# Summing six chunks of squares elementwise before the tensor engine's norm reduction, and loading the root table earlier

## The reference, cut to what matters

```python
def rmsnorm(x, g):
    xf = x.astype(jnp.float32)
    y = xf * lax.rsqrt(jnp.mean(xf * xf, axis=-1, keepdims=True) + NORM_EPS)
    return (y * g.astype(jnp.float32)).astype(x.dtype)

    # per layer l of 2
    h = rmsnorm(x, P['norm1_g'][l]) * (1 + sc1) + sh1
    y = mixer(h)
    x = x + gt1 * y
    h = rmsnorm(x, P['norm2_g'][l]) * (1 + sc2) + sh2
    x = x + gt2 * moe(h, ...)
    # at the end
    y = rmsnorm(x, P['final_g'])
```

## Time and profile before

| what | value |
|---|---|
| median of 3 runs | 1816.75 us (1816.57 to 1817.38) |
| profiled execution, span from its first to its last instruction | 1813.6 us |
| median of the runs less that span | 3.15 us |
| PE busy | 1696.4 us, 94% of the span |
| DVE busy | 861.0 us, 47% |
| ACT busy | 280.8 us, 15% |
| GpSimd busy | 112.4 us, 6% |
| root activations of norms 1, 2, 3, 4 start at | 277.52, 841.25, 1240.05, 1804.23 us |

### The profile page before, as it was taken

The page is one execution under the profiler, slowest core; times in us unless marked ns, Lnnn a source line. Parts: engine busy times, 40 slices in busy tenths (PEclk is TensorE's granted clock), DMA queues, the critical chain, the costliest instruction groups (busy, mean ns, idle before and its releaser), DMA issues.

```text
span 1813.6 us, 25634 instructions
## 1 busy us (share of the span) xinstructions
PE 1696.4 (94%) x9272; PEld 971.4 (54%) x9272; DVE 861.0 (47%) x2513; ACT 280.8 (15%) x645; POOL 112.4 (6%) x115
## 2 busy tenths in 40 slices
PE   5999998999999999988999888878999999999996
PEld 2664576544444444435776877756544444444443
DVE  3206425455545554435672664335445554555444
ACT  2134313100100010003112112102100010001001
POOL 0000001000000000000000322000100000000000
PEclk9999789999999999998999899779999999999998
DMA  9967853699999999994331000033889999999993
GB/s 390 335 257 298 319 209 134 228 421 419 420 419 417 409 419 420 419 406 168 124 132 70 1 1 1 3 150 121 307 338 419 419 420 411 407 419 419 420 420 135
DMA packets 81235, 528.08 MB, mean 291 GB/s; under 512 B 13104, under 2 KB 13632, under 8 KB 20400
## 3 DMA queue, kind: packets, MB, share of 16 engines
q1 hardware_dynamic: 68256, 496.14, 67.0%
q0 software_dynamic: 9024, 20.03, 3.0%
q10 hardware_dynamic: 3824, 10.20, 1.6%
HBM read 533.04 MB, written 5.86 MB: 297 GB/s over the span
## 4 chain that ended last, share of the span: by engine, by line
PE 84%; DMA 8%; DVE 4%; issue 2%; ACT 1%; POOL 0%; SPq 0%; ACTq 0%; DVEq 0%
PE ps L665 21%; PE ps L463 14%; PE ps L709 12%; PE ps L692 11%; DMA ring<-in_wexp 4%; DMA arena<-in_wexp 3%; PE ps L649 3%; PE ps L426 3%; PE ps L612 2%; DVE arena L1267 2%; PE ps L922 1%; PE ps L435 1%; PE ps L925 1%; PE ps L443 1%; PE ps L532 1%
## 5 line engine op out<-in xcount | busy, mean ns | idle before, releaser
L1273 DVE SCALAR_TENSOR_TENSOR x<-ps,mod,x 128x256 f32<-128x256 f32 (+1 forms) x1024 | 329.1, 363 | 189.3 <-PE ps L709 120.3
L665 PE MATMUL ps<-arena 128*32 128x512 f32 (+2 forms) x1456 | 309.1, 609 | 8.4 <-DMA arena<-in_wexp 8.3
L709 PE MATMUL ps<-arena 128*128 128x288 f32 x960 | 264.8, 417 | 6.4 <-DVE x L1273 4.2
L709 PEld LDWEIGHTS ps<-arena 128*128 128x128 f32 x960 | 172.0, 189 | 139.6 <-issue 94.2
L665 PE MATMUL ps<-ring,arena 128*64 128x512 f32 (+1 forms) x976 | 211.4, 597 | 2.1 <-DMA arena<-in_wexp 2.1
L463 PE MATMUL ps<-h,ring 128*128 128x288 f32 x768 | 196.5, 417 | 2.1 <-ACT h L1022 2.1
L463 PEld LDWEIGHTS ps<-h,ring 128*128 128x128 f32 x768 | 149.0, 195 | 45.5 <-issue 4.2
L665 PEld LDWEIGHTS ps<-arena 128*32 128x32 f32 (+2 forms) x1456 | 92.6, 128 | 150.7 <-issue 150.2
L1267 DVE TENSOR_TENSOR arena<-ps,arena 128x256 f32<-128x256 f32 (+6 forms) x153 | 56.1, 373 | 211.5 <-issue 171.6
L692 PE MATMUL ps<-ring,arena 128*64 128x512 f32 (+2 forms) x624 | 134.4, 620 | 11.2 <-DMA ring<-in_wexp 11.2
L1590 DVE COPY arena<-ps 128x512 f32<-128x512 f32 x60 | 41.5, 692 | 172.2 <-PE ps L692 167.0
(11 more groups left out here) (273 smaller groups left out, 1640.1 us busy)
## 6 DMA issues: line engine op xcount, KB each, us to landing
arena<-in_wexp SPq DMA_DIRECT2D x210, 1024.0 KB, 23.3
ring<-in_wexp SPq DMA_DIRECT2D x180, 1024.0 KB, 23.1
ring<-in_wmod SPq DMA_DIRECT2D x48, 1024.0 KB, 9.6
ring<-in_win SPq DMA_DIRECT2D x26, 1024.0 KB, 4.9
ring<-in_wout SPq DMA_DIRECT2D x8, 1024.0 KB, 4.8
h_rows<-arena ACTq DMA_DIRECT2D x4, 512.0 KB, 2.6
x<-in_x ACTq DMA_DIRECT2D x1, 1152.0 KB, 16.1
out_y<-h SPq DMA_DIRECT2D x2, 576.0 KB, 2.8
```

Source lines behind the costliest of these rows:

```text
L665: last = mm(ps[2][w, :], xgT[:, r % 2, 4 * q + k, w], unit(("gu", l, s0 + i, q))[:, k * 512:(k + 1) * 512], start=(q == 0 and k == 0), sto ...
L709: mm(ps[ADD_BANKS[c]][:, 0:T], yb[:, r % 2, c * 128:(c + 1) * 128], onehot[:, r % 2, :], start=True, stop=True).then_inc(sem["add_ps"], 1)
L1273: return V.scalar_tensor_tensor(out=o, in0=a, scalar=s, in1=b, op0=op0, op1=op1)
```

## The change

There are two edits.

1. In norms 1 to 4 the squares of chunks 0 to 5 (`SUMMED = 6`) are added elementwise into `rms`, and PE reduces three operands in place of eight: first `rms`, then the squares of chunks 6 and 7. In norms 1 and 3 the five additions are made by DVE, each behind the square of its chunk in `residual`. In norms 2 and 4 GpSimd makes them, behind its last fetch; each waits for the square of its chunk and, from the second on, for its own previous addition (semaphore `sqp`). The fifth raises `sqa`, for which PE waits.
2. In norms 2 and 4 the root's table load moves from behind the eight squares on ACT to ahead of them. In norms 1 and 3 it stays.

```diff
+SUMMED = 6
@@
             def sum_squares(k):
 
-                for c in range(KC):
+                if k:
+                    pe.wait_ge(sem["sqa"], k)
+                    mm(ps[SS_BANK[k]][:, 0:T], ones, rms[:, :], start=True, stop=False)
+                for c in range(SUMMED if k else 0, KC):
                     pe.wait_ge(sem["sq"], KC * k + c + 1)
-                    last = mm(ps[SS_BANK[k]][:, 0:T], ones, h[:, c, :], start=(c == 0), stop=(c == KC - 1))
+                    last = mm(ps[SS_BANK[k]][:, 0:T], ones, h[:, c, :], start=(k == 0 and c == 0), stop=(c == KC - 1))
                 last.then_inc(sem["ss"], 1)
@@ ACT
             def norm_root(k):
-                if k:
+                if k in (1, 3):
                     warm(ACT.Sqrt)
@@ ACT, end of moe(l)
+                warm(ACT.Sqrt)
                 for c in range(KC):
                     act.wait_ge(sem["add_x"], KC * (B + NR - 1) + c + 1)
                     A(h[:, c, :], x[:, c, :], ACT.Square).then_inc(sem["sq"], 1)
@@ DVE, residual
                     square(i)
+                    if 0 < i < SUMMED:
+                        dve.wait_ge(sem["sq"], KC * (2 * l + 1) + i + 1)
+                        L(tt(rms[:, :], h[:, 0, :] if i == 1 else rms[:, :], h[:, i, :], ALU.add),
+                          "sqa" if i == SUMMED - 1 else None)
@@ GpSimd, end of moe(l)
+                for c in range(1, SUMMED):
+                    po.wait_ge(sem["sq"], KC * (2 * l + 2) + c + 1)
+                    if c > 1:
+                        po.wait_ge(sem["sqp"], (SUMMED - 2) * l + c - 1)
+                    po.tensor_tensor(rms[:, :], h[:, 0, :] if c == 1 else rms[:, :], h[:, c, :], ALU.add)\
+                        .then_inc(sem["sqp" if c < SUMMED - 1 else "sqa"], 1)
```

More of the change, by code:

```diff
@@ L155 @@
 SLOT, NTH, BEFORE = slots_of(UNITS)
-SEMS = """ld_small ld_rest ld_att ld_state st_mix st_small st_out w_used mod_row mod_t cond lamn lame lam sq ss rms hs h
+SEMS = """ld_small ld_rest ld_att ld_state st_mix st_small st_out w_used mod_row mod_t cond lamn lame lam sq sqa sqp ss rms hs h
  proj_ps proj_ev v_ps v_ev v_ev0 pad conv hst gate_ps gate_e lru_a lru_w ya
```

## The result

| | changed kernel | kernel before, same chip |
|---|---|---|
| median of the runs | 1811.01 us (6 runs, 1807.59 to 1812.35) | 1816.66 us (6 runs, 1815.28 to 1818.4) |
| ratio, with its 95% interval | 0.9965 [0.9954, 0.9975] | |
| span of the profiled execution | 1810.6 us | 1813.6 us |
| PE busy | 1688.5 us | 1696.4 us |

The change makes the kernel faster, as forecast. The ratio puts the gain at 1816.75 x 0.0035 = 6.4 us where 4.5 were expected (the two medians are 5.65 apart), with an interval from 4.5 to 8.4 us that just reaches the forecast. The time that the ratio gives, 1810.4 us, is at the low end of the range that was stated. The profiled execution took 1812.35 us for a span of 1810.6. That shifts no difference, only the way from span to run.

The account below looks back on a forecast made before the run. The prediction put the reduction on the path in all four norms, PE itself the limit in norms 1 and 3. Gains of 3.8 and 0.7 us took the median from 1816.75 to 1812.25 us, range 1810.4 to 1815.4.

Parts of the forecast that it names:

- Norms 1 and 3: PE limits the reduction; five matmuls fewer, DVE's additions free, eighth square late next: 1.9 us gained each, 3.8 together.
- Norms 2 and 4: GpSimd's addition chain, then three matmuls: 0.35 us gained each, 0.7 together; bounds per norm 0.8 loss to 0.7 gain.
- The gap between two dependent additions: On GpSimd in norms 2 and 4: taken as 0.09 us, with 0.38 as the upper bound.
- the six entries: PE's three matmuls behind GpSimd's sum in norms 2 and 4: 1.70 us.
- rival C: Clock behind norms: low stretch comes and ends earlier, 1810.75 us, chance 0.11; or one stretch is added, 1813.85, 0.06.
- The sum: All terms: span 1813.6 - 3.8 - 0.7 = 1809.1 us; median 1816.75 - 4.5 = 1812.25, 0.25% less.
- What carries to the end: Work behind the norms, including the MoE weight stream, moves with them, so their gains reach the end.
- Rival B: GpSimd's chain in norms 2 and 4 has gaps near 0.38 us, losing 0.8 each: 1814.55 us, chance 0.12.
- Rival D: Gain of norms 1 and 3 swallowed in the MoE by the weights' stream; only 0.7 stays: 1816.05 us, chance 0.05.
- Rival E: GpSimd and DVE block each other in norms 2 and 4, 2.8 us later each: 1818.55 us, chance 0.04.
- The table load: Root's load on ACT in norms 2 and 4: already hidden, moving it ahead of the squares gains nothing and costs 0.

Follow-up runs that it names:

- pool_norms: Kernel before with GpSimd's sums in norms 2 and 4 only, table load ahead of the squares there; 1816.61 us (11 runs), ratio 0.9995.
- again: The changed kernel run once more, unaltered; 1809.48 us (7 runs), ratio 0.9957 to the kernel before.
- table_behind: The changed kernel with the root's table load back behind the eight squares in all norms; 1809.37 us in one run.
- before_look: The kernel before, without an edit, run for one more trace; 1815.17 us in one run, beside 1817.0 for the kernel before.
- norm3_only: Kernel before with DVE's sum in norm 3 only; 1813.96 us (12 runs), ratio 0.9983.
- dve_norms: Kernel before with DVE's sum in norms 1 and 3 only, table load behind the squares; 1809.27 us (5 runs), ratio 0.9950.
- norm1_only: Kernel before with DVE's sum in norm 1 only; 1813.95 us (12 runs), ratio 0.9984.
- sum_five: Changed kernel, but in norms 2 and 4 GpSimd sums five chunks and PE takes squares 5, 6, the sum, then 7; 1810.10 us, repeated 1808.82.

## Why the prediction was right and wrong

**Norms 1 and 3: right, to 0.04 us.** Forecast 1.94 and 1.93, taken as 1.9; measured 1.90 in each, in every trace that has the sum there. What was named as late next, the eighth square, is what PE waits for (0.26 us), and the root starts 277.76 - 276.46 = 1.30 us behind that square's start. DVE's additions cost nothing: they lie in its idle time, as said, of which 2.25 us are left behind an addition.

**Norms 2 and 4: the right picture with the wrong numbers.** This is one of two terms that were mis-sized: forecast a gain of 0.7, measured 0.13 - 0.31, a loss of 0.18, in the first trace, a gain of 0.04 and a loss of 1.0 in the two repeats, and a gain of 0.25 in `pool_norms`. Two parts of it can be told apart. The gap between two dependent additions is 0.14 to 0.15 us and not the 0.09 of the row behind ACT: five additions take 4.55 us (833.91 to 838.46), not 4.31. That takes 0.24 of the 0.35 in each norm, and `pool_norms`, where nothing else is off, has 0.12 to 0.13 left. The other part is the six entries, forecast at 1.70. In the ten norms of this form they took 1.72 us five times (norm 2 of the first trace, norm 2 of `again`, both in `pool_norms`, norm 4 of `table_behind`) and 1.93 to 2.49 us the other five times, among them 2.16 in norm 4 of the first trace. The granted clock of that one shows it:

```profile
1797.00:1799.00 2.00, 0.01 (x1) 0.01 (x1) 1.06 (x4) 1.10 (x3) 1.65 (x3) 1.00 0.00 0
1799.00:1801.20 2.20, 2.15 (x6) 1.12 (x6) 0.00 (x0) 0.01 (x1) 0.00 (x0) 0.76 0.00 0
```

The clock falls from 1.00 to a mean of 0.76 just behind the two microseconds in which PE waited for GpSimd. The working had this idle time (1.8 us) but used it only for rival C and not in this term. But `pool_norms` idles 2.04 us ahead of the same entries and runs them in 1.72, so the idle time alone does not decide it.

**The sum.** The direct terms come to 3.6 us of gain, against 4.5 forecast. By them alone the gain would have been forecast too large; it was forecast too small.

**The clock, rival C: the step that failed.** "What carries to the end" let all later work move with the norms as it stood, with the idle DMA rows as the only reason, and so priced the clock behind a norm at 0; the better half of C, 1.5 us, had a chance of 0.11. The runs show in its place that a shifted reduction does not carry the stretches at the lower clock along. At norm 3 this is worth 0.55 to 0.58 us in nine of ten traces with the end moved, and costs 0.79 in the tenth (`table_behind`). Behind norm 1, the time from the router to 310 us is 0.3 to 0.65 us shorter in all traces with the sum there, and within 0.12 of before in `before_look`, `pool_norms` and `norm3_only`. Together it is 0.9 to 1.2 us in the usual case. The mechanism that was given for C, a low stretch that comes earlier, while PE is idle anyway, and so ends earlier, is not what gave the gain: at norm 3 the first stretch did come earlier, but it was twice as long and cost 1.15 us, and the gain came from a later one that went away.

The Trainium skill (TensorE: Matmul & The Clock Gate, "What's actually happening") says that the clock follows how busy PE has lately been, as seen by a monitor that runs freely and does not start with the kernel. The trace agrees with the two levels; the third way of `table_behind` behind norm 3 and the two ways behind norm 1, with the same program, are what a monitor with its own phase would give, though no run here sets that phase, and this stays an argument.

**What stays open.** This step explains about one microsecond and not the whole excess. 3.6 and about 1.0 make 4.6 us, and 6.4 were measured, with an interval from 4.5 to 8.4. That interval just holds 4.6. For `dve_norms` 3.8 and 1.0 make 4.8, where 9.1 were measured, 6.4 at the least and 7.3 by the averages from 0.951 on, so there at least 1.6 us have no place in these terms. The first MoE stage (310 to 820 us) is 0.6 to 0.8 us shorter in three traces with norm 1's sum (`dve_norms`, `norm1_only` and the first of the changed kernel), but 0.0 to 0.6 longer in five others and 3.1 longer in one, so a single trace cannot carry this. (The three are those with 7.78 behind norm 1.) The likeliest place is one that the stages so far pass over, the DeltaNet layer. In the four traces whose norm 1 is untouched its length is within 0.1 us of 390.6; in the ten where norm 1's end is moved, earlier or later, it is within 0.25 in four, longer by 6.3 to 6.6 in four and shorter by 1.7 and 3.9 in two. The wide scatter of `norm1_only` beside `norm3_only` fits this. But the kernel before has such executions too (one at 1811.65, ten at a low clock), and no run tells how often each length comes with either kernel, so it is not shown that this makes up the excess. What fixes where the low stretches fall is open too, and with it how much of the excess is theirs.

**Rival B, a slow chain on GpSimd:** the gap is 0.14, between the value taken (0.09) and the bound (0.38); nearer to the former: against the forecast it costs 0.24 and not 1.15 in each norm.

**Rival D, the gain swallowed by the stream of weights:** not borne out. `dve_norms`, which has only the gain of norms 1 and 3, is faster by at least 6.4 us, and in the trace of `norm1_only` the MoE stage behind norm 1 is not longer by 1.90 but 0.8 us shorter.

**Rival E, DVE and GpSimd shut each other out:** refuted for these forms. Eight update entries of `x` (four chunks) took 2.67 us beside GpSimd's additions in the changed kernel and 2.68 in `dve_norms`, which has none, and the additions took 0.79 to 0.80 us, like the product in the earlier trace rows. The rule of the Trainium skill that was cited (SBUF — State Buffer, "Who interferes with whom") agrees with this if the scalar column doesn't count as an input, which is what these rows show for this form.

**The table load:** right, it is worth nothing in this kernel. In norm 4 it ends with its small activation 0.67 us before the first square, and behind the squares it is hidden too.

## What to carry to other kernels

Take work off a reduction where PE itself is the limit, and put the sum where it is ready before PE asks: in norms 1 and 3 five matmuls less gave the 1.9 us that the rows promised. Where the operands arrive one by one, a chain on a slower engine is only as good as its pitch, so give it the early chunks, let the tensor engine take the late ones directly, and leave one matmul behind the last operand; `sum_five` gained 1.17 us in a norm in which the chain over six chunks gained 0.13 or lost. And when work is shifted by two microseconds between idle gaps of PE, do not price what follows at nothing: here one stage behind a norm gave 0.6 us or took 0.8, and in single traces a whole layer was 3.9 us shorter or 6.6 longer. Take several traces, and compare them stage by stage.

## What the runs showed of the hardware

- A GpSimd addition of 128x288 fp32 takes 0.79 us, starts 0.09 us behind ACT's end, and follows an addition that it depends on after 0.14 to 0.15 us: 0.94 from start to start.
- The same 24 matmul entries take 6.09 or 7.78 us, the same 16 router entries 5.5 to 7.1, by where the stretches at the lower clock fall. Behind norm 3 thirteen of fourteen traces have one of two pairs, 5.78 with 7.78 or 6.9 with 6.09, each repeated to 0.04 us; behind norm 1 one and the same program had 5.47 with 7.78 in one trace and 6.91 with 6.09 in another.
- 63 executions of the unaltered kernel before lie between 1811.65 and 1824.17 us, with mean granted clocks of 0.948 to 0.956; the ten up to 0.950 are 4.7 us longer on average, more than the whole direct effect of this change.
